# The third out product of a fused network, whole or by token block, ahead of 512 expert gathers

## The reference, cut to what matters

```python
merged = gates[:, :, 0] * (y_rw @ w_br_rwkv[i]) + gates[:, :, 1] * (y_mla @ w_br_mla[i])
x = x + merged @ w_out[i]                        # 1024 x 1024
x = x + peer_ffn(rmsnorm(x, g_ffn[i]), peer_w_q[i], peer_sub_keys[i], peer_u[i], peer_v[i])
...
def block(hb):                                   # 128 tokens, twice
    q = (hb @ w_q).reshape(n, 8, 2, 128)         # 8 heads, 2 halves
    s = jnp.einsum('nhcd,hckd->nhck', q, sub_keys)
    sc, ix = lax.top_k(s, 16)
    cand = sc[:, :, 0, :, None] + sc[:, :, 1, None, :]
    cidx = ix[:, :, 0, :, None] * 128 + ix[:, :, 1, None, :]
    top, pos = lax.top_k(cand.reshape(n, 8, 256), 16)
    eidx = jnp.take_along_axis(cidx.reshape(n, 8, -1), pos, axis=-1)
    gate = jax.nn.softmax(top, axis=-1)
    act = jax.nn.gelu(jnp.einsum('nhed,nd->nhe', expert_u[eidx], hb), approximate=False)
    return jnp.einsum('nhe,nhed->nd', (gate * act), expert_v[eidx])
```

## Time and profile before

| | |
|---|---|
| median of 3 runs | 2273.82 us |
| the profiled execution, its own time | 2269.86 us |
| span of its instructions | 2268.1 us |
| PE busy in the span | 2014.0 us (89%) |
| DVE busy | 1275.9 us (56%) |
| ACT busy | 805.3 us (36%) |
| POOL busy | 647.8 us (29%) |
| moved by DMA | 489.60 MB, of which gathers 268.53 MB |
| mean granted TensorE clock | 0.962 of full |

### The profile page before, as it was taken

The page is one execution under the profiler, slowest core; times in us unless marked ns, Lnnn a source line. Parts: engine busy times, 40 slices in busy tenths (PEclk is TensorE's granted clock), DMA queues, the critical chain, the costliest instruction groups (busy, mean ns, idle before and its releaser), DMA issues.

```text
span 2268.1 us, 35190 instructions
## 1 busy us (share of the span) xinstructions
PE 2014.0 (89%) x14082; PEld 1629.9 (72%) x14082; DVE 1275.9 (56%) x2328; ACT 805.3 (36%) x1336; POOL 647.8 (29%) x671
## 2 busy tenths in 40 slices
PE   7999989999999999999998999986778767767876
PEld 7999979999999988999777898872333323323424
DVE  5554635555554664554656453385656566656544
ACT  5344335444443554443654332222211122112212
POOL 0000010000000100000001322047777777777772
PEclk9999999999999999999999999998899889989999
DMA  9554506554655523654305101579999999999994
GB/s 310 190 182 130 186 1 223 194 179 148 199 172 166 168 76 106 224 172 150 112 19 158 49 21 39 169 256 377 353 379 379 358 376 386 375 363 363 380 378 170
DMA packets 254878, 489.60 MB, mean 216 GB/s; under 512 B 13936, under 2 KB 174224, under 8 KB 254624
## 3 DMA queue, kind: packets, MB, share of 16 engines
q0 software_dynamic: 73888, 268.53, 31.3%
q1 hardware_dynamic: 177104, 214.32, 29.1%
q10 hardware_dynamic: 3760, 5.02, 0.7%
HBM read 486.74 MB, written 1.05 MB: 215 GB/s over the span
## 4 chain that ended last, share of the span: by engine, by line
PE 68%; POOL 12%; DMA 8%; issue 5%; DVE 5%; ACT 3%; POOLq 0%; DVEq 0%; ACTq 0%
PE bank L790 67%; POOL arena_sb L2856 10%; DMA con_sb<-peer_v,arena_sb 3%; DMA arena_sb<-peer_u,arena_sb 3%; POOL con_sb L2856 2%; DMA arena_sb<-peer_v,arena_sb 1%; DVE parts_sb L2141 0%; PE bank L981 0%; DVE xT_sb L2205 0%; DVE parts_sb L2136 0%; DVE sq_sb L2722 0%; ACT parts_sb L1658 0%; DMA xT_sb<-xT 0%; DMA ring_sb<-w_in 0%; DMA ring_sb<-ffn_w_gate 0%
## 5 line engine op out<-in xcount | busy, mean ns | idle before, releaser
L790 PE MATMUL bank<-arena_sb 64*64 64x64 f32 (+7 forms) x3692 | 510.6, 320 | 149.3 <-ACT arena_sb L2089 114.3
L790 PE MATMUL bank<-xh_sb,parts_sb 128*128 128x256 f32 x3328 | 605.4, 284 | 19.5 <-DVE parts_sb L2136 16.2
L790 PEld LDWEIGHTS bank<-arena_sb 64*64 64x64 f32 (+4 forms) x3692 | 297.6, 160 | 354.4 <-issue 210.3
L790 PEld LDWEIGHTS bank<-xh_sb,parts_sb 128*128 128x128 f32 x3328 | 514.7, 190 | 25.9 <-issue 24.9
L790 PE MATMUL bank<-xl_sb,parts_sb 128*128 128x256 f32 x1808 | 509.9, 282 | 0.0
L2722 DVE CUSTOM_DVE_ANT_0 sq_sb<-arena_sb 128x1024 f32<-128x1024 f32 x256 | 309.5, 1224 | 259.5 <-DMA arena_sb<-peer_u,arena_sb 256.8
L2136 DVE TENSOR_TENSOR parts_sb<-ring_sb,parts_sb 128x2048 fp32r<-128x2048 f32 x132 | 298.6, 2289 | 173.1 <-ACT parts_sb L1644 173.1
L790 PEld LDWEIGHTS bank<-xl_sb,parts_sb 128*128 128x128 f32 x1808 | 343.7, 190 | 0.0
L2856 POOL DMA_INDIRECT arena_sb<-peer_u,arena_sb x256 | 278.1, 1086 | 185.3 <-DVE arena_sb L2650 101.6
L1644 ACT ACTIVATE parts_sb<-ring_sb 128x2048 fp32r<-128x2048 f32 x132 | 248.0, 1910 | 69.7 <-PE bank L790 68.5
L790 PE MATMUL bank<-h_high_sb,parts_sb 128*128 128x256 f32 x1408 | 255.8, 282 | 0.0
(11 more groups left out here) (280 smaller groups left out, 1859.3 us busy)
## 6 DMA issues: line engine op xcount, KB each, us to landing
ring_sb<-ffn_w_gate SPq DMA_DIRECT2D x44, 1024.0 KB, 5.4
ring_sb<-ffn_w_up SPq DMA_DIRECT2D x44, 1024.0 KB, 6.6
ring_sb<-ffn_w_down SPq DMA_DIRECT2D x44, 1024.0 KB, 5.0
ring_sb<-w_in SPq DMA_DIRECT2D x17, 1024.0 KB, 6.0
ring_sb<-w_in_ab SPq DMA_DIRECT2D x12, 1024.0 KB, 5.2
ring_sb<-w_out SPq DMA_DIRECT2D x12, 1024.0 KB, 5.2
ring_sb<-w_in_cd SPq DMA_DIRECT2D x12, 1024.0 KB, 5.3
ring_sb<-peer_w_q SPq DMA_DIRECT2D x8, 1024.0 KB, 5.3
```

Source lines behind the costliest of these rows:

```text
L790: return pe.matmul(dst, lhsT, rhs, start=start, stop=stop_, skip_group_check=loose)
```

## The change

The third out product, the norm behind it, the token transposes and the queries of heads 0 to 2 are made by token block. `out_block(0)` (64 matmuls of 128 columns) and `norm_block(0)` go first, then queries of heads 0 and 1 for the first 128 tokens and their transposes, and only then `out_block(1)`, the third head's queries of block 0, `norm_block(1)` and the queries of heads 0 to 2 of block 1. Head 3 is made whole ahead of the weighted rows. Heads 4 to 7 now all stand inside units 0 to 3, one half after row 7 and one after row 15 of each (before: the last two heads, one half after each of the units 0 to 3). `out_block(0)` releases no `wo` slot, `out_block(1)` does.

DVE adds block 0 to the residual and norms it, does `best(0)` and `best(1)`, then adds block 1, makes dots 0 to 2, norms block 1, and goes on with dot 3. `MG` moves to the place of two `peer_v` buffers, and the squares of block 1 lie in a third, so POOL waits for the second sum of squares (`("ssq7", 1)`) ahead of unit 1.

```diff
-        MG = view(9984, 8, T)
+        MG = view(19856, 8, T)
+        SQ7 = [sq[:, 0:4, :].rearrange("p a b -> p (a b)").rearrange("p (k t) -> p k t", k=KC), view(21904, KC, P)]
...
-        FIRST_HEADS = 6
-        LATE = {0: ("query", 12), 1: ("query", 13), 2: ("query", 14), 3: ("query", 15), 4: ("ple", 0), 5: ("ple", 4)}
+        EARLY_HEADS = 3
+        BOTH = 2
...
+        LATE = {(u, e): ("query", 4 + u, c) for u in range(4) for e, c in ((7, 0), (15, 1))}
+        LATE[4, 15], LATE[5, 15] = ("ple", 0, 0), ("ple", 4, 0)
...
-                out_product(2, MG)
+
+            def out_block(tb):
+
+                for m in range(KC):
+                    k, label = at["wo", 2] + m // 2, ("y", 2, 2 * tb + m // 4)
+                    b = fill_begin(pe, label) if m % 4 == 0 else bank[fill_of[label][0]]
+                    if tb == 0 and m % 2 == 0:
+                        have(k)
+                    for kk in range(KC):
+                        if tb + m == 0:
+                            pe.wait_ge(S("merged"), kk + 1)
+                        ins = mm(b[:, (m % 4) * P : (m % 4 + 1) * P], slot(k, KC, 256)[:, kk, (m % 2) * P : (m % 2 + 1) * P],
+                                 MG[:, kk, tokens_of(tb)], kk == 0, kk == KC - 1)
...
+                    if tb and m % 2:
+                        owed[0] += 1
...
-                for m in range(2 * FIRST_HEADS):
-                    query(m)
-                    if m == 1:
-                        tokens()
+                queries(0, 0)
+                queries(1, 0)
+                tokens(0)
+                out_block(1)
+                queries(2, 0)
+                norm_block(1)
+                for h in range(EARLY_HEADS):
+                    queries(h, 1)
+                tokens(1)
+                queries(EARLY_HEADS, BOTH)
...
+                act.preload_act_table_set("natural_log_exp_and_others")
+                squares7(0)
+                root7(0)
+                queries_out(0, 0)
+                queries_out(1, 0)
+                tokens_out(0)
+                queries_out(2, 0)
+                squares7(1)
+                root7(1)
...
+                residual_block(0)
+                norm_block(0)
                 best(0)
                 best(1)
-                for j in range(4):
+                residual_block(1)
+                for j in range(2):
                     emptied(dve, ("htok", j))
                 for u, (tb, h) in enumerate(UNITS):
                     for e in range(16):
                         n = 16 * u + e
+                        if n == 3:
+                            norm_block(1)
...
             for u in range(17):
+                if u == 1:
+                    emptied(pool, ("ssq7", 1))
                 if u < 16:
                     pool.wait_ge(S("rows_known"), u + 1)
```

More of the change, by code:

```diff
@@ L1457, in branches_out @@
                     branch_part(0, m)
-                out_product(2, MG)
-            def experts():
[L1461 to L1466, removed]
+            def out_block(tb):
[9 more added lines that the diff above has]
+                                 MG[:, kk, tokens_of(tb)], kk == 0, kk == KC - 1)
+                        if kk == 0:
+                            release(ins)
+                    if m % 4 == 3:
+                        fill_end(ins, label)
+                    if tb and m % 2:
+                        owed[0] += 1
@@ new lines, in norm_block, with scores @@
+            def norm_block(tb):
+                b = fill_begin(pe, ("ssq7", tb))
+                for k in range(KC):
+                    if k % 4 == 0:
+                        pe.wait_ge(S("squares7"), 2 * tb + k // 4 + 1)
+                    ins = mm(b[:, 0:P], C("ones", P), SQ7[tb][:, k, :], k == 0, k == KC - 1)
+                    if k == 0:
+                        release(ins)
+                fill_end(ins, ("ssq7", tb))
+            def experts():
+                def scores(h, part):
+                    b = fill_begin(pe, ("sc", h, part))
+                    for c in range(2):
+                        emptied(pe, ("pq", h, part, c))
+                    for tb in blocks_of(part):
@@ L1483, in query @@
                         if kk == 0:
                             release(ins)
-                    fill_end(ins, ("pq", m))
+                    fill_end(ins, ("pq", h, part, c))
                     if c == 1:
[L1487 to L1495, removed]
+                        owed[0] += part > 0
+                        scores(h, part)
@@ L1496, in tokens, with queries @@
+                def queries(h, part):
+                    for c in range(2):
+                        query(h, part, c)
+                def tokens(tb):
+                    for i in range(2):
+                        b = fill_begin(pe, ("htok", 2 * tb + i))
+                        for k in range(4):
+                            ins = pe.transpose(b[:, k * P : (k + 1) * P], xn[:, 4 * i + k, tokens_of(tb)], ident)
+                            if i + k == 0:
                                 release(ins)
-                        fill_end(ins, ("htok", j))
+                        fill_end(ins, ("htok", 2 * tb + i))
@@ L1620, in _ @@
             branches_out()
-            norm(7)
+            out_block(0)
+            norm_block(0)
             experts()
@@ L2089, in experts @@
                         act.activation(DG[q % ND], ident, ACT.Copy, scale=WT[:, tb, 16 * h + e : 16 * h + e + 1]).then_inc(S("diag_ready"), 1)
-                    if u in LATE:
-                        kind, first = LATE[u]
-                        if kind == "query":
-                            query_out(first)
-                        else:
-                            for m in range(first, first + 4):
-                                b = take(act, ("pp", m))
-                                give(act.activation(PLE[:, m, :], b[:, 0:T], ACT.Copy), ("pp", m))
+                        if (u, e) in LATE:
+                            kind, first, c = LATE[u, e]
+                            if kind == "query":
+                                query_out(first, BOTH, c)
+                            else:
+                                for m in range(first, first + 4):
+                                    b = take(act, ("pp", m))
+                                    give(act.activation(PLE[:, m, :], b[:, 0:T], ACT.Copy), ("pp", m))
                 squares(8, 1)
```

121 lines of the change are left out of this document (80 added, 41 removed).

## The result

The changed kernel took **2264.01 us**, median of 12 runs (2248.97 to 2277.23), beside 2273.39 us for the kernel before in 12 runs on the same chip (2269.14 to 2286.18). The ratio is 0.9949, 95% interval 0.9929 to 0.997: a gain of 6.8 to 16.1 us, within 1%. Two further sets of runs of the changed kernel stand among the experiments; they gave 9.5 and 12.5 us. Two single executions among all that follow, one of dots_first (2902 us) and one of the kernel before (3340 us), ran at a mean granted clock of 0.65 and 0.56 and stand in no ratio. That the median is the forecast to a hundredth is luck, since the interval is 9 us wide. What the forecast can be held to is its steps.

A forecast was written before the change was run, and what follows sets the result against it. POOL's issuing of gathers was taken as the pace. Gather 17 going out 11.1 us earlier, less 1 us for queries in the units, gave 10 us: 2260 profiled, plus 3.96 for the median, 2264 us; range 2256 to 2274.

The forecast's parts named there:

- The gathers' start: From merged branches to the first gather: shorter PE and norm work lets gather 0 go out 17.8 us earlier.
- Out product of block 0: On PE ahead of the first norm: 128 records of 128 columns take 14.6 us instead of 27.8, saving 13.2.
- the rival without shorter records: On PE: 128-column records cost the 256-column price, so gain is near nothing, 2273 us; chance 0.03.
- Norm: From the last residual to the first normed chunk: half width at the root saves some 0.2 us of 4.41.
- Norm out and query: DVE's normed chunks and the first half queries on PE: about 4.2 us instead of 7.8, saving 3.6.
- The second norm's wait: DVE between dots 2 and 3 waits about 4 us for block 1's root; with the norm itself, cost 6.1 us.
- the lengthening: POOL's gather issues take over 0.94 us while dots run, some 93 us in all; could move time 3 us either way.
- the middle queries: Extra half queries on PE inside units 0 to 3, mostly absorbed in waits for rows; cost 1 us in all.
- Bytes: DMA at 373 GB/s, not POOL, paces the gathers; gain only 4 us, time 2270 us; chance 0.15.
- Held gathers: Queries in the units delay the diagonals and POOL waits for row buffers; loss of 5 us, 2279; chance 0.09.
- Late weights: Head 2's weight fetch lands 3.5 us late and delays block 1's norm; gain 7, 2267 to 2268; chance 0.10.
- Second norm free: Block 1's root is ready sooner and no unit slips; gain 15 to 17 us, time 2258; chance 0.08.

The follow-up runs named there:

- dots_first: norm_first with block 1's residual put behind dot 2 and its norm behind dot 6 of unit 0; 2261.89 us, 0.9975 of the kernel before.
- out_together: Changed kernel with block 1's out product directly behind block 0's, ahead of the first norm; 2268.55 us, 0.9993 of the kernel before.
- norm_first: Changed kernel with block 1's sum of squares ahead of head 2's query on PE and ACT; 2251.89 us, repeated at 2256.84 us.
- half_dots: Changed kernel with each dot over the first 512 of 1024 elements, gathers still whole; 2211.53 us, 0.9739 of the kernel before.
- half_both: half_dots with each gather also moving only 512 elements a row; 2219.01 us, 0.9783 of the kernel before.
- queries_ahead: Changed kernel with heads 4 and 5 queried ahead of unit 0's diagonals, one half query left per unit 0 to 3; 2263.17 us, 0.9961 of before.

## Why the prediction held, step by step

**The gathers' start** (predicted 17.8 us earlier; measured 65.7 - 47.2 = 18.5 at full clock, 17.1 in the profile after). *Out product of block 0*: 41.71 - 28.37 = 13.3 where 13.2 stood; the price of 0.114 us a record was right (14.46 us for the 128 records of the second half are 0.113), and the rival without shorter records fell. *Norm*: from residual to norm 3.35 us (1468.90 to 1472.25) in place of 4.41, 1.06 saved where I had 0.2. I had halved only the root, and the sums of squares are halved too. *Norm out and query*: at full clock 1475.88 to 1480.40 in out_together, 4.52 us, 3.2 saved where 3.6 stood. *Scores*: 0.8, as said. The sum is 18.4.

**Dot 0** follows gather 0 by 11.0 us, before by 11.1, and DVE waited 1.02 us for block 1's product, as the forecast had it. **The second norm's wait** was 4.44 us where "about 4" stood, and the norm came 18.95 us behind gather 0 where the working gave 19.3. norm_first shows the cause to be the one named, the queue behind head 2's query. POOL's two waits, at gathers 7 and 10, are there; a third at gather 13 (2.13 us) I had not named, and it stems from the same late dots. **Gather 17** came 11.8 us earlier at full clock (10.4 in after), predicted 11.1.

**From gather 17 on**, the three profiles of the changed kernel give 707.3, 692.6 and 701.8 us, mean 700.6, the two of before 703.0 and 700.4, mean 701.7. These means hide the scatter of the lengthening. Less the part of it that falls into the stretch, the three are 615.8, 614.7 and 614.6, against 614.6 and 614.6 before: the middle queries cost 0.1 us or less in two executions and 1.2 in the one with the wait in unit 14, where I had 1. The tail is 39.8 us in the mean against 38.0, with 37.7 and 38.6 in norm_first, which has the same tail: scatter, as far as five profiles can tell.

**Weights.** The third `wq` slot was issued at 1489.00 and landed 6.6 us later, 3.7 us before its query (1499.30) where 1.4 was forecast; the next three took 16.2 to 18.4 us and nobody waited for them.

**Rivals.** Bytes: refuted by half_dots and half_both. By the Trainium skill (SBUF — State Buffer, A bandwidth-pool intuition that's wrong) HBM gives a core about 358 GB/s, which its row gets by sharing a stack's 716 between two cores. Here one core ran, and the 404 GB/s over 300 us are above that figure, so the measurement decides and the share is no bound here. Held gathers: the mechanism exists and needs more than the change puts there (no wait of POOL for PE in units 1 to 5 in its three profiles); queries_ahead shows it with 7.63 us, and norm_first with 1.6 and 3.1 us, when the same queries meet earlier gathers. Late weights: no. Second norm free: no, but norm_first frees DVE of the wait for it and brings gather 17 forward by 4.5 us, of which 2 to 3.4 are left at the last gather.

**The working's own slips** are small: the issue of 1.78 us ended 0.8 us after the dot beside it (1548.72 against 1547.91), not 0.9, and from gather 17 on there are 494 issues, not 495.

**What was mis-sized** is the noise. "That alone can move the time by 3 us either way" stood beside the lengthening; in five profiles of the two kernels it runs from 81.8 to 95.4, 13.6 us, as large as the gain. The start of the products came 12.3 us later with the clock's pieces ahead of it, and I had no term for them. "The profiled execution would read 2260" failed by 17 us (2277.23): 12 are this start, some 3 the stage behind gather 17 with the largest lengthening of all profiles, 1 the tail and 1 the piece at 1473; the median carried the forecast.

## What to carry to other kernels

Where a long stage starts on a small part of what comes before it, run that part's whole chain first, even at a price in PE records; then check on every engine's queue what the other part now stands behind, because the engine at the far end (here DVE, for a root on ACT behind a query on PE) gives some of the gain back. Compare profiles from a mark just ahead of the change, not by their ends: here single runs of one kernel scatter by 17 to 28 us, and the distance from gather 0 to gather 17 shows 4.5 us plainly. Where two resources look full at once, shorten the work of one without touching the other, and see which full share goes away.

## What the runs showed that I had not expected

- **Two "full" resources, one of them not**: DMA at 0.99 of its time and 371 GB/s went on to 1.02 and 404 GB/s as soon as the issues came faster. A share of 0.99 was no proof of a bound.
- **Shorter dots lengthen issues less**: dots of 1.22 us cost 78 to 95 us over 512 issues, dots of 0.69 us 21 us, or 52 with smaller gathers. The Trainium skill (SBUF — State Buffer, Who interferes with whom) has DVE and GpSimd share a port pair, locked for an instruction; the fall with the dots' length agrees, though no run here isolates the port.
- **The start of a stage moved by up to 13 us under the same code**: 1427.4 to 1440.5 in twelve profiles, with TensorE granted 0.90 and 0.86 in the late one's stretches ahead of it and 1.00 in the early one's.
- **A fetch among gathers**: 1 MB took 6.6 us at the start of the gathers and 11.6 to 18.4 us once they ran in full, against 5.3 in the median of before. The cover that counts is the one at the end of the queue, not the first one's.
